# Two decoder layers on one Trainium2 core: rotary halves exchanged by DMAs of GpSimd instead of matmuls, constant tables loaded in five pieces, adaptation sums and probability transposes at other places

## The reference, cut to what matters

```python
for l in range(DEPTH):                                   # DEPTH = 2
    mod = silu(c) @ ada_w[l] + ada_b[l]                  # 1024 -> 6144
    sh_m, sc_m, g_m, sh_f, sc_f, g_f = split(mod, 6)
    h = modulate(rmsnorm(x, mix_pre_g[l]), sh_m, sc_m)
    t = h @ w_in[l]                                      # all three branches and their gates
    y = (sigmoid(gate_lru) * (rglru(...)     @ lru_wo[l])
       + sigmoid(gate_ret) * (retention(...) @ ret_wo[l])
       + sigmoid(gate_mla) * (mla(...)       @ mla_wo[l])) @ w_out[l]
    x = x + g_m * rmsnorm(y, mix_post_g[l])
    h = modulate(rmsnorm(x, ffn_pre_g[l]), sh_f, sc_f)
    x = x + g_f * rmsnorm(conv_glu(h), ffn_post_g[l])    # 1024 -> 2 x 2816 -> 1024

def apply_rope(x, cos, sin):        # retention q, k; latent attention q and the shared key
    x1, x2 = halves(x)
    return concat(x1 * cos - x2 * sin, x1 * sin + x2 * cos)
```

## Time and profile before

| | |
|---|---|
| median of 3 runs | 958.68 us (957.09 to 959.09) |
| profiled execution, its own time | 959.5 us |
| its span, first to last instruction | 957.7 us |
| TensorE busy | 931.6 us, 97% |
| VectorE busy | 731.3 us, 76% |
| ScalarE busy | 522.7 us, 55% |
| mean granted clock | 0.998 of full speed |

### The profile page before, as it was taken

How to read it: one execution, slowest core, us unless ns; L and a number is a source line. 1 busy time by engine, 2 the same in 40 slices (tenths; PEclk the granted TensorE clock), 3 DMA queues, 4 the chain that set the end, 5 groups by cost and what they waited for, 6 DMA issues and landing times.

```text
span 957.7 us, 17447 instructions
## 1 busy us (share of the span) xinstructions
PE 931.6 (97%) x6840; PEld 863.5 (90%) x6840; DVE 731.3 (76%) x988; ACT 522.7 (55%) x693; POOL 43.7 (5%) x85
## 2 busy tenths in 40 slices
PE   6999999999999999999999999999999999999997
PEld 6889899889987999999979999989999799999996
DVE  4969968877787878887786877887768776676666
ACT  4445756445557655454673475743446675554553
POOL 0000000100000000000000000000000000000000
PEclk9999999999999999999999999999999999999999
DMA  9995757775583676766645775767666455655451
GB/s 351 327 287 194 230 200 262 239 240 200 186 295 113 231 254 245 256 241 199 203 170 169 252 240 189 248 210 236 207 230 233 163 176 179 216 175 179 146 202 44
DMA packets 134427, 206.36 MB, mean 215 GB/s; under 512 B 6497, under 2 KB 104801, under 8 KB 134241
## 3 DMA queue, kind: packets, MB, share of 16 engines
q1 hardware_dynamic: 122704, 162.08, 51.5%
q0 software_dynamic: 11520, 41.95, 12.0%
q10 hardware_dynamic: 144, 1.51, 0.5%
HBM read 204.47 MB, written 1.05 MB: 215 GB/s over the span
## 4 chain that ended last, share of the span: by engine, by line
PE 80%; DVE 11%; DMA 3%; ACT 2%; issue 2%; SPq 1%; DVEq 0%; ACTq 0%; POOLq 0%
PE banks L1705 73%; DVE w_lo L1097 3%; DVE adw L1090 2%; DMA h<-in_ada_rows 1%; DMA raw<-in_w_in 1%; DMA adw<-in_ada_rows 1%; SPq L463 1%; PE banks L1995 1%; PE banks L1985 1%; PE banks L1988 1%; ACT h_hi L656 1%; PE banks L1816 1%; DVE EF L1607 1%; PE banks L1862 0%; PE banks L2004 0%
## 5 line engine op out<-in xcount | busy, mean ns | idle before, releaser
L1705 PE MATMUL banks<-h_lo,w_hi 128*128 128x256 f32 x1504 | 426.0, 283 | 5.9 <-DVE h_lo L1158 2.2
L1705 PE MATMUL banks<-h_hi,w_lo 128*128 128x256 f32 x1504 | 420.7, 280 | 0.0
L1705 PE MATMUL banks<-h_hi,w_hi 128*128 128x256 f32 x1504 | 420.4, 280 | 0.0
L1705 PEld LDWEIGHTS banks<-h_lo,w_hi 128*128 128x128 f32 x1504 | 283.3, 188 | 10.9 <-issue 4.9
L1705 PEld LDWEIGHTS banks<-h_hi,w_lo 128*128 128x128 f32 x1504 | 283.5, 188 | 2.3 <-issue 1.4
L1705 PEld LDWEIGHTS banks<-h_hi,w_hi 128*128 128x128 f32 x1504 | 283.4, 188 | 0.0
L1097 DVE TENSOR_TENSOR w_lo<-raw,w_hi 128x2048 fp32r<-128x2048 f32 x96 | 219.4, 2289 | 47.0 <-ACT w_hi L598 46.5
L598 ACT ACTIVATE w_hi<-raw 128x2048 fp32r<-128x2048 f32 x96 | 182.7, 1912 | 103.6 <-PE banks L1705 82.0
L1607 DVE SCALAR_TENSOR_TENSOR EF<-banks,par,EF 128x254 f32<-128x254 f32 (+1 forms) x176 | 76.8, 478 | 57.6 <-ACT EF L949 51.8
L1631 DVE TENSOR_TENSOR w_lo<-raw,w_hi 128x2048 fp32r<-128x2048 f32 x42 | 96.0, 2286 | 21.1 <-ACT w_hi L968 21.1
L968 ACT ACTIVATE w_hi<-raw 128x2048 fp32r<-128x2048 f32 x42 | 80.4, 1913 | 36.7 <-PE banks L1705 36.7
(11 more groups left out here) (275 smaller groups left out, 1210.8 us busy)
## 6 DMA issues: line engine op xcount, KB each, us to landing
raw<-in_w_in SPq DMA_DIRECT2D x52, 1024.0 KB, 5.8
raw<-in_ffn_w_up SPq DMA_DIRECT2D x44, 1024.0 KB, 5.1
adw<-in_ada_rows POOLq DMA_DIRECT2D x80, 512.0 KB, 4.9
raw<-in_ffn_w_down SPq DMA_DIRECT2D x22, 1024.0 KB, 4.9
raw<-in_w_out SPq DMA_DIRECT2D x8, 1024.0 KB, 7.3
raw<-in_ret_wo SPq DMA_DIRECT2D x4, 1024.0 KB, 6.7
raw<-in_lru_wo SPq DMA_DIRECT2D x4, 1024.0 KB, 6.9
raw<-in_mla_wo SPq DMA_DIRECT2D x4, 1024.0 KB, 7.1
```

The source lines that it names most:

```text
L1705: ins = MM(ps, lhs, rhs, start=first and n == 0, stop=last and n == 2)
```

## The change

It has these parts:

- **Rotation.** The six rotation matmuls of a layer are gone, and with them the constant matrices. The inverse frequencies of the second half of each head carry a minus sign, so that the sine part has its sign already; GpSimd's queue then exchanges the halves by DMAs from SBUF to SBUF: 4 for each of the four q and k pairs (32 partitions each), 8 for the latent key and 8 for the latent query (16 partitions each). VectorE adds `lat` or `ptb` in place of the bank. TensorE waits (`heads_taken`) only until VectorE has read the banks; it waits for the finished q and k (`rope`) before `ret_score(0)`, for the latent key and query before `mla_scores(0)`. `rotary_key_sum` stands behind split 15, `rotary_q_sum` behind `ret_low(1)`.
- **Tables.** Five pieces of 128x384 to 128x640 go through SyncE's queue behind the blocks 5 to 9. `wbd` is loaded by GpSimd's queue.
- **Sums.** Those behind the splits 7 to 12 are gone from there; the same number is added in the merge steps 4, 6, 8 and 9.
- **First layer only.** `angles` of the latent part and the three stages of softplus stand one to three blocks earlier.
- **Attention.** In the steps 2, 4 and 6 `mla_transpose` stands behind the product, `mla_av` between the two tiles of the next step's gate, and ScalarE splits its block before `transposed`.
- Both `head_scales` stand behind both value products.

```diff
-    inv_ret = (ROPE_THETA ** (-np.arange(0, 64, 2) / 64.0))[f % 32][:, None]
+    inv_ret = ((ROPE_THETA ** (-np.arange(0, 64, 2) / 64.0))[f % 32] * np.where(f % 64 < 32, 1.0, -1.0))[:, None]
...
-    parts = [ident, ones, inv_ret, inv_mla, eps, q_eps, tiny, center, mean64, rotation(64), rotation(32), *decay, mask]
+    parts = [ident, ones, inv_ret, inv_mla, eps, q_eps, tiny, mean64, *decay, mask]
...
@@ sync
-                    if j == 4:
-
-                        sp.wait_ge(wbd_zero, 1)
...
-                                sp.dma_start(wbd[64 * b:64 * b + 64, m, :, 64 * b:64 * b + 64], blockw).then_inc(wbd_in.s, 16)
+                    if l == 0 and 5 <= j < 5 + len(TABLES):
+                        a, b = TABLES[j - 5]
+                        sp.dma_start(cst[:, a:b], consts[:, a:b]).then_inc(tables_in, 16)
...
@@ gpsimd
-            load(0, 0)
-            load(1, 1)
-            with pool.Fori(0, TILES // 2 - 1) as it:
...
+            def next_tiles(first, last):
+
+                for n in range(first, last):
+                    pool.wait_ge(ada_red.s, n - 1)
+                    load(n, n % 2)
+
+            def halves_turned(dst, src, half, landed_sig):
+
+                for p in range(0, P, half):
+                    q = p ^ half
+                    pool.dma_start(dst[p:p + half], src[q:q + half]).then_inc(landed_sig.s, 16)
+
+            def turn(l, i):
+
+                two = slice(2 * (i % 2), 2 * (i % 2) + 2)
+                pool.wait_ge(rot_t.s, rot_t.at(l, i + 1))
+                if i >= 2:
+                    pool.wait_ge(rope.s, rope.at(l, i - 1))
+                halves_turned(lat[:, two, :], tmp[:, two, :], 32, turn_in[i % 2])
+
+            for l in range(L):
+                t = 2 * NT * l
+                for i in range(4):
+                    turn(l, i)
+                    if l == 0 and i == 1:
+                        load(0, 0)
+                        load(1, 1)
+                pool.wait_ge(kt_t.s, kt_t.at(l, 1))
+                halves_turned(lat[:, 1, :], lat[:, 0, :], 16, kt_in)
+                next_tiles(t + 2, t + 8)
+                pool.wait_ge(qt_t.s, qt_t.at(l, 1))
+                halves_turned(turned_q, rot_tmp, 16, qt_in)
+                next_tiles(t + 8, t + NT)
...
@@ vector
-            mixer_sums = {j: n for n, j in enumerate(range(7, 21))}
-            merge_sums = (2, 1, 2, 1, 2, 1, 2, 1, 1, 1, 2, 2)
+            mixer_sums = {j: n for n, j in enumerate(range(13, 21))}
+            merge_sums = (2, 1, 2, 1, 3, 1, 3, 1, 3, 3, 2, 2)
...
@@ tensor
-                    MM(PS[:, (2, 4, 5, 0)[i], :], rot_r, flat2(tmp, i % 2), start=True, stop=True).then_inc(rot_ps.s, 1)
-
-
-                rotate(0)
-                rotate(1)
+                pe.wait_ge(v_ev.s, v_ev.at(l, 4))
                 two_tiles(l, J[("lx", 0)], 3)
-                rotate(2)
                 two_tiles(l, J[("lx", 1)], 1)
-                rotate(3)
-
-                pe.wait_ge(rope.s, rope.at(l, 2))
+                heads_taken(1)
                 two_tiles(l, J[("c", 0)], 4)
...
-                pe.wait_ge(kt.s, kt.at(l, 1))
+                pe.wait_ge(kt_t.s, kt_t.at(l, 1))
+                pe.wait_ge(kt_c.s, kt_c.at(l, 1))
                 two_tiles(l, J[("g", 1)], 2)
...
-                    merge_gate(m)
+                    if m > 2 and m % 2 == 1:
+                        merge_gate(m, (0,))
+                        mla_av(m // 2 - 1)
+                        merge_gate(m, (1,))
+                    else:
+                        merge_gate(m)
                     if m % 2 == 0:
+                        merge_product(m)
                         mla_transpose(m // 2 - 1)
-                        merge_product(m)
-                        mla_av(m // 2 - 1)
```

More of the change, by code:

```diff
@@ L59, in constants @@
     same_head = (f[:, None] // 64 == f[None, :] // 64).astype(np.float64)
-    center = ident - same_head / 64.0
     mean64 = same_head / 64.0
     ones = np.ones((P, P))
-    def rotation(dim):
-        half = dim // 2
-        r = np.zeros((P, P))
-        for m in range(P):
-            if m % dim < half:
-                r[m + half, m] = -1.0
-            else:
-                r[m - half, m] = 1.0
-        return r
     t = np.arange(seq)[None, :]
@@ L282, in trunk_kernel @@
         inv_ret, inv_mla, eps, q_eps, tiny = (piece(2 * P + i, 1) for i in range(5))
-        center, mean64, rot_r, rot_m = (piece(NFIRST + P * i) for i in range(4))
-        c0 = NFIRST + 4 * P
+        mean64 = piece(NFIRST)
+        c0 = NFIRST + P
         decay = cst[:, c0:c0 + HEADS * T].rearrange("p (h t) -> p h t", h=HEADS)
@@ L289, in trunk_kernel @@
         col = {**COL, "-8sp": P + 120, "8sp": P + 124}
+        TABLES = [(NFIRST, c0 + T), *((c0 + T + 2 * i * T, c0 + T + 2 * (i + 1) * T) for i in range(HEADS // 2 - 1)),
+                  (c0 + (HEADS - 1) * T, NCONST)]
         def PC(l, name, i=0, n=1):
@@ L328, in trunk_kernel @@
         g_th, g_ev = sig("g_th", 2), sig("g_ev", 2)
-        rot_ps, rot_t, rot_c, rope = sig("rot_ps", 4), sig("rot_t", 4), sig("rot_c", 4), sig("rope", 4)
+        rot_t, rot_c, rope = sig("rot_t", 4), sig("rot_c", 4), sig("rope", 4)
+        turn_in = [sig(f"turn_in{i}", 128) for i in range(2)]
         rs_ps, rs_p, rs_av = sig("rs_ps", 8), sig("rs_p", 8), sig("rs_av", 8)
@@ L545, in _, with recurrence_weights @@
             pool.wait_ge(ada0_used, len(ON_PE))
-            pool.wait_ge(hi_ready.s, hi_ready.at(0, 4))
-            load(0, 0)
-            load(1, 1)
-            with pool.Fori(0, TILES // 2 - 1) as it:
-                for slot in range(2):
-                    pool.wait_ge(ada_red.s, it * 2 + (1 + slot))
-                    pool.sem_inc(tick, 1)
-                    load(it * 2 + (2 + slot), slot)
+            pool.wait_ge(wbd_zero, 1)
+            def recurrence_weights(l):
+                for m, name in enumerate(("lru_wa", "lru_wx")):
+                    for b in range(2):
+                        blockw = A[name][l].rearrange("(i b) h k -> b h i k", b=2)[b]
+                        pool.dma_start(wbd[64 * b:64 * b + 64, m, :, 64 * b:64 * b + 64], blockw).then_inc(wbd_in.s, 16)
@@ L745, in _ @@
                     split_block(l, j)
-                    if l == 0 and j in (4, 8):
-                        sines((0, 2)[j // 8])
+                    if l == 0 and j in (4, 6):
+                        sines(j - 4 if j == 4 else 2)
+                    if l == 0 and j == 7:
+                        softplus_exp()
+                    if l == 0 and j == 8:
+                        softplus_log()
                 for i in range(2):
@@ L914, in _ @@
                     gate(m)
-                    if m % 2 == 0 and 2 <= m <= HEADS:
+                    if m == HEADS:
                         transposed(m // 2 - 1)
                     split_block(l, j + RING + m % 2)
+                    if m in (2, 4, 6):
+                        transposed(m // 2 - 1)
                     if m == 6:
@@ L1324, in _ @@
                 mixer_split(l, 5)
+                if l == 0:
+                    angles(sinm, cosm, inv_mla)
+                    softplus(0)
                 rope_parts(1)
@@ L1838, in _ @@
                 pe.wait_ge(lx_c.s, lx_c.at(l, 12))
-                pe.wait_ge(rope.s, rope.at(l, 4))
+                heads_taken(3)
                 lru_gate(0)
@@ L1867, in _ @@
                 two_tiles(l, J[("g", 0)], 4)
-                pe.wait_ge(kt_t.s, kt_t.at(l, 1))
-                MM(PS[:, 2, 0:T], rot_m, lat[:, 0, :], start=True, stop=True).then_inc(kt_ps.s, 1)
+                pe.wait_ge(rope.s, rope.at(l, 4))
                 pe.wait_ge(lr_ev.s, lr_ev.at(l, 1))
@@ L1944, in head_means @@
                 def head_means(i):
+                    if l == 0 and i == 0:
+                        pe.wait_ge(tables_in, 16 * len(TABLES))
                     pe.wait_ge(rv_sq.s, rv_sq.at(l, i + 1))
```

68 lines of the change are left out of this document (33 added, 35 removed).

## The result

| | before | after |
|---|---|---|
| median | 958.88 us (4 runs, 957.09 to 959.22) | 978.5 us (4 runs, 977.39 to 978.71) |
| profiled execution: span | 957.7 us | 976.4 us |
| mean granted clock | 0.998 | 0.979 |

The ratio is 1.0206, with a 95% interval of 1.0188 to 1.0224: the changed kernel is 19.6 us slower. The forecast was 969.3 us, 10.6 more than before, in a range of 958 to 980. The direction and the range held; the loss was almost twice as large.

A forecast was written before the change was run, and what follows sets the result against it. TensorE, busy 97% of the span, was taken as the bound. Gains of 16.8 us against 27.4 lost gave 10.6 more: 970.1 on the profiled execution, 969.3 us at the median, range 958 to 980.

The forecast's parts named there:

- the key: TensorE's wait for the rotated latent key: 2.2 us and 1.7 of clock gone, 1.4 back for `lat_rc`, net 2.5 us gained.
- the probabilities: TensorE's waits at steps 2 and 6, four places, go with transposes behind the product: 3.1 us gained.
- The rotations' 9.7 us: Rotation matmuls of q, k, latent query and key leave TensorE's path in two layers: 9.7 us gained.
- the 16.8 us: Sum of all forecast gains: rotations 9.7, tables and `wbd` 1.5, wait for the key 2.5, transposes 3.1 us.
- The rival of late halves: Exchanged halves come late if small transfers take 8.8 us: up to 5 us a layer more, 974 to 980; chance 0.12.
- The step on the sums: Moved adaptation sums wait for tiles in two buffers and delay splits in merge steps 6 to 9: 27.4 us lost.
- product 10: TensorE's wait for its block behind VectorE's sums of steps 8 and 9: 2.0 + 2L, 10.8 us a layer.
- M: Start of `merge(8)` on VectorE, 254.19 in the earlier profile, from which the sums and splits are timed.
- L: Landing time of a 512 KB adaptation tile after issue: rows give 3.7 to 8.8 us, median 5.0; taken as 4.4.
- Step 8's probabilities: Step 6's third sum ends late, so the probabilities reach TensorE's transposes about 1.2 us late in each layer.
- The clock: Work at low clock behind the new pause of TensorE: 1.7 us lost in each layer.
- the rival that the two cancel: With L = 3.7, no clock loss and 18.2 us of gains, losses equal gains: 959.3 us, no difference; chance 0.06.

The follow-up runs named there:

- experiment 4: Changed kernel with the twelve adaptation tiles feeding the sums of merge steps 4 to 9 cut to 64 KB: 963.9 us, ratio 1.0061.
- The fastest kernel: Changed kernel with first tiles early, never three sums in a row, step 9's splits ahead of its sums, reciprocal ahead of split 14's sum: 940.8 us, ratio 0.9812.

## Why the prediction was right in direction and half the size

**What held.** TensorE bounds the kernel, and what comes off it comes off the time. The waits that were to go are gone: 1.5 us for the tables' split, 2.2 for the key with 1.2 for `lat_rc` in its place, 3.1 for the probabilities. The rotations' 9.7 us are right to about 2. How much of the 16.8 us shows depends on the order around them: with the sums at their old places 10.1 at the median and 13.9 in the profiled execution, with the sums spread 14.8 without the transposes. The halves came late nowhere: one wait of VectorE of 1.5 us in the changed kernel, hidden. The estimate for the transfers was 3.7 us; in the first layer the exchanges into `lat` landed in 1.6 to 6.5 us, median 5.5, with VectorE's slack to hide it. The rival of late halves fell.

**The step on the sums.** The chain of waits was right: which sums would stand idle, which split would be late, that product 10 would wait about 9 us, that step 8's transposes would wait. The reason given for a short landing was not: VectorE's own late split stopped the loads, not TensorE's wait (experiment 4). Four sizes were off:

- *Product 10.* With M = 249.97 in the first layer, the last sum ended at M + 15.8 and the split at about M + 18.0; the formula with the measured L of 3.88 and 3.82 gives M + 16.6 and M + 18.8. The 0.82 us from the end of a sum to the issue was 0.38 here (252.45 to 252.83), and it counts twice. And L was 3.85, not 4.4. In the second layer the two landings were 3.7 and 3.75, and the fourth sum waited 0.7 us for its tile, which the formula does not have. So 18.2 in place of 21.6 us: 3.4 too much.
- *Step 8's probabilities.* This is the term that was missed by most. One L of 4.4 was used for all places, though the argument for it was made for the steps 8 and 9 alone. At step 6 nothing had stopped the loads, the DMA engines were full, and L was 7.21, within the 3.7 to 8.8 of the earlier trace rows. That is 2.8 us later, less 0.44 for the shorter gap ahead of the issue: the transposes waited 3.6 us and not 1.2, in both layers: 4.8 us too little.
- *The clock.* 1.7 us a layer was taken from the earlier trace rows, where the pause was 1.6 us long, and for one pause a layer. (That figure took the windows whole; with busy time in them, 3.38 x 0.11 + 5.00 x 0.23, it is the 1.5 us of the books.) There were two, and behind the long one more work ran at the low clock: 1.5 + 2.7 us in the first layer. Together 7.4 in place of 3.4: 4.0 too little.
- *Small waits* for `w_lo`: 1.9 us where none was forecast. "At step 4 the delay falls into a gap" was right but for a wait of 0.7 us in the first layer and 1.2 in the second.

-3.4 + 4.8 + 4.0 + 1.9 is 7.3 us, less 0.2 at the start 7.1, of the 8.1 between the sum of 10.6 and the 18.7 between the spans; the last 1.0 us is the busy time left over in the books. The formula for product 10 was right where its own landings are put in; the loss was underrated because step 6 was given the landing time of another stretch, and because the clock was counted for one pause a layer.

Two slips in the prediction change nothing: 0.84 plus half of 0.06 is 0.87, not 0.86, and the rival that the two cancel leaves out step 8's probabilities, 0.5 us a layer by the prediction's own formula.

## What to carry to other kernels

With two buffers, the third use in a row costs issue plus landing plus work here, however low the average load of the DMA engines is; two such rows, one behind the other, add up. The same argument gives the (n+1)th use for n buffers, but no run here has another number of them. A table with no row longer than the buffers was worth more (951.3 us against 978.5, with the loads placed to fit) than the matmuls that the change removed. Put what another engine waits for ahead of work that nobody waits for, above all ahead of work that can itself wait. And take a transfer's landing time from the rows of the stretch in question: the same tile took 3.9 or 7.2 us, by what else was moving.

## What the runs showed of the hardware

- An eighth of the bytes saved 1.7 us of 3.9 where the DMA engines had been at 0.59, and 1.4 of 7.2 where they had been at 1.06: with the engines at 1.04, a transfer of 64 KB took 5.8 us.
- A pause of TensorE of 3.6 us cost 1.4 to 1.5 us more in work at a granted clock of 0.66 to 0.72, one of 8.8 us 2.7 us, one of 9.4 us in the second layer 1.9 us: the longer pause did not cost more, and no run here settles what sets it. The fastest kernel has no window below full clock between its first 60 us and its last 15. Less waiting did not always cost less: the kernel with rows of three in the steps 10 and 11 had 2.9 us less of waits than the changed kernel, in six pauses in place of four, and 2.8 us more of lost clock.
- GpSimd took 484 to 527 ns to issue each DMA of the exchanges of halves, while VectorE was busy for 20.7 of 23 us around those of the first layer. The rule that the prediction named from the Trainium skill (SBUF — State Buffer, section SBUF: two separate sides), by which a two-port operation of VectorE keeps GpSimd from writing descriptors, left no mark in these rows. No row tells whether any operation that VectorE ran there is of that kind, so they do not test the rule itself.
